# An mLSTM layer in fp32: a finished head's norm spread over the next head's products, and the spreads of the gate rows in pairs

## The reference, cut to what matters

```
b     = cumsum(log_sigmoid(f))                      # a row over time
D[t,s]= b[t] - b[s] + i[s]   for s <= t, else -inf   # reversed time for the second direction
m[t]  = max(max_s D[t,s], b[t] + m_before)
S     = (q @ k^T) * exp(D - m)
h     = (S @ v) / max(|sum_s S|, exp(-m))
out   = rms_norm((h_forward + h_backward) * sigmoid(o)) * silu(z)
```

## Time and profile before

| | us |
|---|---|
| median of 3 runs | 3587.09 (3586.32 to 3589.01) |
| the profiled execution | 3585.12, of it 3583.3 span |
| TensorE busy | 3475.2 (97%) |
| VectorE busy | 1887.5 (53%) |
| ScalarE busy | 1160.5 (32%) |
| GpSimd busy | 921.1 (26%) |

### The profile page before, as it was taken

One profiled execution on the slowest core, in us unless ns is written; L12 is line 12 of the kernel. 1 busy time (PEld: TensorE's weight loads), 2 busy tenths in 40 slices (PEclk: granted clock), 3 DMA queues, 4 the chain that ended last, 5 costly groups with the idle time before them and its releaser, 6 DMA issues.

```text
span 3583.3 us, 53959 instructions
## 1 busy us (share of the span) xinstructions
PE 3475.2 (97%) x22362; PEld 2341.8 (65%) x22362; DVE 1887.5 (53%) x3530; ACT 1160.5 (32%) x2185; POOL 921.1 (26%) x736
## 2 busy tenths in 40 slices
PE   8999999999999999999999999999999999999998
PEld 4555555665668887777777756444555545878887
DVE  3555553445444354666666653454767733554543
ACT  3444442222231123333333322765555521110100
POOL 2222211222210013555555410223445420000000
PEclk9999999999999999999999999999999999999999
DMA  5121211111112111111111111221101011221221
GB/s 229 65 86 65 86 36 50 44 36 36 36 48 94 71 65 60 48 48 48 48 38 47 54 71 59 84 77 62 49 31 48 17 74 59 106 94 72 87 81 56
DMA packets 29555, 229.78 MB, mean 64 GB/s; under 512 B 3072, under 2 KB 6784, under 8 KB 9728
## 3 DMA queue, kind: packets, MB, share of 16 engines
q1 hardware_dynamic: 29312, 226.33, 17.0%
HBM read 224.22 MB, written 2.10 MB: 63 GB/s over the span
## 4 chain that ended last, share of the span: by engine, by line
PE 88%; DVE 6%; ACT 2%; issue 2%; DMA 1%; POOL 0%; SPq 0%; DVEq 0%; ACTq 0%; POOLq 0%
PE bank L1295 12%; PE bank L1608 11%; PE bank L1514 7%; PE bank L1950 7%; PE bank L1602 4%; PE bank L1977 4%; PE bank L1729 3%; PE bank L1868 2%; PE bank L1420 2%; PE bank L1688 2%; PE bank L1695 2%; PE bank L1453 2%; PE bank L1242 2%; PE bank L1914 2%; PE bank L1658 1%
## 5 line engine op out<-in xcount | busy, mean ns | idle before, releaser
L1295 PE MATMUL bank<-xT,ring 128*128 128x384 f32 x896 | 319.2, 492 | 2.2 <-ACT Y L2092 2.1
L3615 POOL TENSOR_TENSOR ring<-ring 128x512 f32<-128x512 f32 x112 | 146.9, 1327 | 398.0 <-DMA ring<-in_w 396.3
L3653 POOL TENSOR_TENSOR ring<-ring 128x512 f32<-128x512 f32 x128 | 171.5, 1346 | 285.1 <-DMA ring<-in_w 284.3
L1608 PE MATMUL bank<-Y,ring 128*128 128x384 f32 (+1 forms) x768 | 240.7, 457 | 0.0
L1295 PE MATMUL bank<-hT,ring 128*128 128x384 f32 x672 | 239.5, 490 | 0.0
L1295 PEld LDWEIGHTS bank<-xT,ring 128*128 128x128 f32 x896 | 162.6, 191 | 109.4 <-issue 12.9
L3679 POOL TENSOR_TENSOR arena<-arena 128x512 f32<-128x512 f32 x112 | 184.0, 1643 | 170.9 <-PE bank L1658 155.6
L1608 PE MATMUL bank<-hT,ring 128*128 128x384 f32 (+1 forms) x576 | 184.8, 457 | 9.2 <-DVE arena L3053 8.5
L1729 PE MATMUL bank<-hT,ring 128*128 128x512 f32 x384 | 180.7, 605 | 4.7 <-ACT Y L2067 4.7
L1608 PEld LDWEIGHTS bank<-Y,ring 128*128 128x128 f32 x768 | 141.2, 190 | 64.7
L1295 PEld LDWEIGHTS bank<-hT,ring 128*128 128x128 f32 x672 | 122.8, 190 | 79.8 <-issue 12.7
(11 more groups left out here) (588 smaller groups left out, 7458.6 us busy)
## 6 DMA issues: line engine op xcount, KB each, us to landing
ring<-in_w SPq DMA_DIRECT2D x77, 1024.0 KB, 4.8
ring<-in_w SPq DMA_DIRECT2D x35, 2048.0 KB, 8.5
ring<-in_w SPq DMA_DIRECT2D x20, 1280.0 KB, 5.5
ring<-in_w SPq DMA_DIRECT2D x10, 1536.0 KB, 7.2
ring<-in_w SPq DMA_DIRECT2D x8, 1408.0 KB, 5.9
ring<-in_w SPq DMA_DIRECT2D x6, 512.0 KB, 4.0
xT<-in_xT SPq DMA_DIRECT2D x1, 3072.0 KB, 14.7
xT<-in_xT SPq DMA_DIRECT2D x4, 512.0 KB, 6.2
```

The source lines that it names most:

```text
L1295: ins = e.matmul(bank[spot["st", kind, n, at]][:, 0:384], left[:, k], right[:, k], start=first and k == 0, stop=k == 3, skip_group_check=True)
L1608: ins = e.matmul(o, left[:, k], moved, start=first and k == 0, stop=k == 3, skip_group_check=True)
L3615: e.tensor_tensor(s[:, i], l, r, op).then_inc(up("st_s", (kind, n, i)), 1)
L3653: e.tensor_tensor(s[:, i], l, r, op).then_inc(up("gs_s", (kind, n, i)), 1)
```

## The change

`ml_attend` puts the two spreads of a direction in one unit, one directly behind the other: those of direction 1 behind piece 3, those of the next head's direction 0 behind piece 12. `ml_steps` takes a group of the norm only behind every second product.

```diff
-    units[2].append(("ml_bc", h, 1, 0))
-    units[3].append(("ml_bc", h, 1, 1))
+    units[3] += [("ml_bc", h, 1, 0), ("ml_bc", h, 1, 1)]
     if h < 3:
-        units[10].append(("ml_bc", h + 1, 0, 0))
-        units[12].append(("ml_bc", h + 1, 0, 1))
+        units[12] += [("ml_bc", h + 1, 0, 0), ("ml_bc", h + 1, 0, 1)]
...
-        for name, i in turns:
-            made += [(name, h, i)] + (side.pop(0) if side else [])
+        for n, (name, i) in enumerate(turns):
+            made += [(name, h, i)] + (side.pop(0) if side and n % 2 == 0 else [])
```

## The result

| | before | after |
|---|---|---|
| median of 5 runs, us | 3586.32 (3585.66 to 3589.01) | 3598.50 (3597.72 to 3600.43) |
| after / before, 95% interval | | 1.0038 [1.0027, 1.0048] |
| span of the profiled execution, us | 3583.3 | 3596.7 |
| mLSTM stretch, us | 479.1 | 493.5 |

The kernel became 12.2 us slower; forecast were 7.7. The measured time lies 3.7 us above the forecast and 0.5 us above the range. It contains every place that the change touches.

A forecast was written before the change was run, and what follows sets the result against it. TensorE, busy 97% of the span, was taken as the bound. Norm -4.44, direction 1's pairs +4.76 and direction 0's +7.35 gave +7.7 us on the median 3587.1, so 3594.8 us; range 3591 to 3598.

The forecast's parts named there:

- The reading of the bound: Whole kernel: TensorE is busy 97% of the span, so work added in front of it costs in full unless it lands in a wait.
- Part 1: Norm's sums in the mLSTM: v4 stands ahead of the sum, removing a 1.48 us wait in three heads, 4.4 us gained.
- the ring: Ring of two banks in the norm's new order: s1 and s3 were to get no new wait.
- the late `ml_yd`: Second `ml_yd`, queued ahead of the third argument: some 1.7 us of VectorE work slides into idle time, costing nothing.
- Part 2: Direction 1's spreads behind piece 3: second waits for the first's bank copies, 1.19 us more, four heads, 4.8 us lost.
- Part 3: Direction 0's spreads behind piece 12: nothing gained at piece 11, 2.45 us more per pair, three heads, 7.4 us lost.
- The sum: All three parts: -4.44 + 4.76 + 7.35 = +7.7 us, set on the runs' median, 3594.8 us.
- Side-by-side wait absorbed: Part 2's 1.19 us vanish in the wait at piece 11 in three heads: +4.1, 3591.2 us; a tenth.
- No wait for the banks: Copies at the pairs are over in time: -2.0 us in all, 3585.1 us; 8 in 100.
- The norm's wait only moves: Norm's wait goes to s1 or to pieces behind the late `ml_yd`: +12.1, 3599.2 us; 7 in 100.
- The signs: Trace after: no wait at the norm's sum, seven waits of 1.3 to 1.4 us at spreads, three of 1.9 at masks.

The follow-up runs named there:

- after's two traces: The changed kernel, traced in its first measurement (3598.50 us) and again unchanged on the chip of the experiments (3599.72 us).
- the full rows with a wait of 1.41 us: Changed kernel with spreads as products over all 128 rows and ScalarE copying the second row of a 512-token spread twice: 3600.20 us.
- part 2 alone: Kernel before with only direction 1's two spreads put side by side behind piece 3, four pairs: 3592.02 us.
- part 3 alone: Kernel before with only direction 0's two spreads put side by side behind piece 12, three pairs: 3592.81 us.
- the free banks: Changed kernel with each pair's second spread writing to the unused banks 6 and 7, so it needn't wait for the copies: 3581.11 us.
- part 1 alone: Kernel before with only the norm's groups placed behind every second product, spreads as before: 3579.46 us.
- the best order: Changed kernel with direction 0's pair behind piece 10 instead of 12 and every pair's second spread on banks 6 and 7: 3574.79 us.

## Why the prediction was partly right

**The reading of the bound** held: TensorE is 97% busy before and after, and every place's cost arrived in full.

**Part 1** was right: -4.4 forecast, -4.4 measured alone. The sum starts behind v4 with no wait; the ring gave no new wait at L1410, and the late `ml_yd` cost nothing.

**Part 2** was right as a place: 2.45 us between the starts forecast and seen, +4.8 forecast and +4.8 measured alone. The Trainium skill's sentence on packing (TensorEngine Tiling (Array Packing), PSUM Bottleneck) was the right one to weigh: ScalarE's two copies, 1.09 us, and not TensorE's products set when the second spread starts.

**Part 3** was right as a place too: +7.4 forecast, 9.1 - 1.7 = +7.4 measured. Its two halves are now measured singly, 3.9 for a spread laid bare and 3.5 for standing side by side with the wait for the banks.

**The sum** has the failed step. It added places and priced each product behind a pair at what it took before. There was no term for TensorE's clock. I had the waits of 1.25 us of the norm, behind which the clock did not fall, and took from them, without a word, that a wait of 1.3 us costs 1.3 us. At the pairs it also costs 1.7 us where the clock falls, in one case 3.5: 6.8 us in each of after's two traces. With the +7.7 forecast for the places that makes +14.5 for the stretch, measured +14.4 and +14.3; the runs' medians rose by 12.2 and 13.5.

What separates the pairs from the norm's wait is what runs around the wait. At the norm, products over 128 rows stand on both sides; at the pairs, products over 32 rows. The five traces with a 1.3 us wait between 32-row products show 11 falls at 28 pairs, four of the five at least one. The six traces in which one of the two is missing, or the wait is about half as long, show none at 42 pairs: 128 rows with a longer wait, 32 rows with half the wait, or 32 rows for 2.78 us with none. Seven pairs of one trace could stay at full clock by chance (at 11 in 28, an estimate: 17/28 to the seventh power, 3 in 100), but the clocks of all their runs agree: those six kernels had means of 0.9940 to 0.9946, as before or better, and the three kernels with all seven pairs waiting 1.32 us between 32-row products 0.9918 to 0.9926. Both together are needed, as far as these runs go. How long the wait must be between 0.74 and 1.32 us, and whether other narrow shapes do the same, no run here shows. The Trainium skill has a passage in this direction (TensorE: Matmul & The Clock Gate, A second HAM failure mode: psum-queue depth-cycling): in a bf16 kernel that cycles through banks, TensorE is idle between groups of products for moments, and its clock swings between the levels. This case agrees that the fall comes at a wait for a bank; the full rows with a wait of 1.41 us at a clock of 1.00 show that the wait alone doesn't decide.

**Still open** is which pairs fall. The same pair fell in one trace of after and not in the other, and part 2 alone showed no fall at four pairs that have both the rows and the wait. Nor do the parts' own clock losses clearly add up: over their runs, part 2 alone lost about 1.9 us more than before on the same chip and part 3 alone 1.2 (mean clocks 0.9936 and 0.9938 against 0.9942), both pairs with the norm as before 4.7, and all three parts 6.7 and 7.5. These are means of 5 to 11 runs whose clocks are recorded to 0.001 (3.6 us), so the step from 3.1 to 4.7 can be noise; the step to 7 hardly can. What makes it wasn't found.

**The rivals.** Side-by-side wait absorbed: no, +4.8 arrived. No wait for the banks: no; the free banks show what it would have given, -3.6 and not -2.0. The rival counted two spreads in a row as 1.06 + 0.63, with no edge between them; they take 0.20 less than that. I had weighed there a rule of the Trainium skill (TensorE: Matmul & The Clock Gate, The mechanism), that a weight load overlaps running products only on other rows. These two spreads use the same rows and run with no edge (1.49 us for both), so the measurement decides against it here; the same section also lets a load run ahead into the array's background weight buffer, and that reading fits. The norm's wait only moves: no, part 1 alone gained all of it. That its 3599.2 us lies nearest to the result is luck.

**The signs.** The forecast of the median lay at the bound of 0.2%, and the chance for slower was 0.49; the measured ratio lies clearly above it. With the clock counted it would not have been a close call. The signs named for the trace all came and none of those against it did; none of them looked at the clock.

## What to carry to other kernels

A wait put into a queue of small products can cost more than its length: look at the granted clock of the stretch behind it as well as at the wait, and allow for it in the range if no row of the old trace shows a wait of this length among products of this shape. Before two steps are put side by side, ask what the second one reuses of the first: here, two banks more turned +14 us into -4. And a step that stands in a wait of its engine is free; look for such a wait before moving it, and move other work into it (the best order has -8.4 us where the free banks have -3.6).

## What the runs showed of the hardware

- TensorE's clock fell from its 2.4 GHz to its 1.2 GHz level (granted clock 0.51 to 0.62 over the windows of 3.5 to 7.5 us shown above) behind waits of 1.32 us that had products over 32 rows on both sides, 11 times at 28 pairs; behind waits of 1.41 us among products over 128 rows it stayed at 1.00 seven times in seven. Each fall cost 1.7 us, one of them 3.5.
- Two spreads of 32 rows in a row save 0.40 us against the two apart: the 0.10 us at each of the two inner edges to products over 128 rows, and another 0.20 (1.49 us for 512 and 256 columns of both rows, where apart they take 1.06 + 0.63). A repeat of the same work costs 1.29 us.
- A bank read out by ScalarE is back in TensorE's hands 0.14 us behind the copy's end (809.75 + 1.09 = 810.84, next product at 810.98).
